# One of the two units of each expert matrix is fetched on ScalarE's queue, the other on SyncE's

## The reference

```python
hb = jax.nn.silu(xb @ w_gate[e]) * (xb @ w_up[e])
return (hb @ w_down[e]) * g[:, None].astype(x2.dtype)
```

## Time and profile before

| | us |
|---|---|
| median of 3 runs (1364.02 to 1364.54) | 1364.14 |
| the profiled execution's own time | 1364.34 |
| its span, first to last instruction | 1362.6 |
| PE busy | 1202.1 |
| ACT busy | 267.4 |

### The profile page before, as it was taken

One profiled execution on the slowest core, in us unless ns is written; L12 is line 12 of the kernel. 1 busy time (PEld: TensorE's weight loads), 2 busy tenths in 40 slices (PEclk: granted clock), 3 DMA queues, 4 the chain that ended last, 5 costly groups with the idle time before them and its releaser, 6 DMA issues.

```text
span 1362.6 us, 18400 instructions
## 1 busy us (share of the span) xinstructions
PE 1202.1 (88%) x7496; PEld 787.6 (58%) x7496; DVE 468.2 (34%) x1154; ACT 267.4 (20%) x687; POOL 323.7 (24%) x343
## 2 busy tenths in 40 slices
PE   7999999986856556676899999999999999999997
PEld 6865555452522121222286569999448666999843
DVE  3443434101011010101125646444573224444467
ACT  4313432010000000000224531111013222111100
POOL 5000100000000000000111348878001113987800
PEclk9999998988987787888999999999999999999999
DMA  9643345999999999999997135554343058644400
GB/s 349 196 176 124 124 183 210 425 428 423 429 427 426 430 428 428 430 425 424 407 314 258 39 106 187 173 186 155 128 151 123 0 167 266 207 149 172 155 0 31
DMA packets 101357, 335.82 MB, mean 246 GB/s; under 512 B 6728, under 2 KB 58240, under 8 KB 87069
## 3 DMA queue, kind: packets, MB, share of 16 engines
q1 hardware_dynamic: 98662, 326.33, 62.1%
q0 software_dynamic: 2416, 8.30, 1.7%
q10 hardware_dynamic: 199, 0.06, 0.0%
HBM read 333.59 MB, written 2.86 MB: 247 GB/s over the span
## 4 chain that ended last, share of the span: by engine, by line
PE 71%; DMA 18%; DVE 3%; POOL 3%; ACT 2%; issue 2%; SPq 1%; POOLq 0%; DVEq 0%; ACTq 0%
PE bank L1714 18%; PE bank L892 18%; DMA ring<-in_w_expert_up 11%; PE bank L1764 8%; PE bank L1248 5%; PE bank L1266 4%; DMA ring<-in_w_expert_down 2%; DMA ring<-in_w_expert_gate 2%; PE bank L1872 2%; DMA wide_rows<-in_w_expert_gate 2%; PE bank L1138 2%; PE bank L1685 2%; PE bank L1527 1%; PE bank L1500 1%; PE bank L1055 1%
## 5 line engine op out<-in xcount | busy, mean ns | idle before, releaser
L892 PE MATMUL bank<-wide_rows,ring 128*128 128x256 f32 (+3 forms) x592 | 129.9, 372 | 0.2 <-ACT ring L2014 0.2
L1714 PE MATMUL bank<-R,arena 128*128 128x128 f32 x1056 | 125.1, 275 | 0.0
L1248 PE MATMUL bank<-ring,arena 128*32 128x512 f32 x512 | 79.2, 711 | 49.8 <-DMA ring<-in_w_expert_up 38.5
L1714 PEld LDWEIGHTS bank<-R,arena 128*128 128x128 f32 x1056 | 121.5, 192 | 0.0
L892 PEld LDWEIGHTS bank<-wide_rows,ring 128*128 128x128 f32 (+1 forms) x592 | 107.5, 190 | 19.7 <-issue 3.9
L3189 POOL COPY arena<-w_router 128x256 f32<-128x256 f32 x1 | 0.4, 397 | 476.3 <-PE bank L1248 476.3
L2693 DVE TENSOR_TENSOR arena<-arena,bank 64x512 f32<-64x512 f32 x16 | 11.1, 691 | 294.9 <-ACT arena L2127 294.9
L1248 PE MATMUL bank<-wide_rows,arena 128*32 128x512 f32 x128 | 68.4, 686 | 47.4 <-DMA arena<-in_w_expert_up 35.6
L1714 PE MATMUL bank<-wide_rows,ring 128*128 128x128 f32 x704 | 91.3, 276 | 1.5 <-ACT wide_rows L2112 1.5
L1714 PEld LDWEIGHTS bank<-wide_rows,ring 128*128 128x128 f32 x704 | 84.7, 192 | 2.5 <-ACT wide_rows L2112 2.5
L1266 PE MATMUL bank<-ring,arena 128*32 128x512 f32 x504 | 72.5, 718 | 13.0 <-ACT arena L2130 10.1
(11 more groups left out here) (394 smaller groups left out, 1956.1 us busy)
## 6 DMA issues: line engine op xcount, KB each, us to landing
ring<-in_w_expert_down SPq DMA_DIRECT2D x29, 2048.0 KB, 16.1
ring<-in_ffn_w_in SPq DMA_DIRECT2D x44, 1024.0 KB, 7.8
ring<-in_w_expert_gate SPq DMA_DIRECT2D x16, 2048.0 KB, 25.0
ring<-in_w_expert_up SPq DMA_DIRECT2D x16, 2048.0 KB, 32.4
arena<-in_w_expert_up SPq DMA_DIRECT2D x14, 2048.0 KB, 32.6
ring<-in_ffn_w_out SPq DMA_DIRECT2D x10, 2048.0 KB, 7.8
ring<-in_w_in SPq DMA_DIRECT2D x7, 2048.0 KB, 15.8
arena<-in_w_expert_gate SPq DMA_DIRECT2D x7, 2048.0 KB, 26.5
```

What stands on the lines that cost most here:

```text
L892: last = pe.matmul(dst, lhsT, rhs, start=k == 0, stop=k == len(pairs) - 1)
L1248: last = pe.matmul(bank[e % 2][at:at + SLOTS, :], xg_tile(e % 2, k)[:, SLOTS * r:SLOTS * r + SLOTS], w[r][:, kk, :], start=k == 0, stop=k ...
L1714: last = pe.matmul(up_banks[layer][u % 4][i][:, at * P:(at + 1) * P], weights(k), columns(k), start=k == 0, stop=k == KT // 2 - 1)
```

## The change

From pair 3 on, SP issues only units 0, 2 and 4 of each pair (`of[::2]`, or `of[1::2]` where the list begins with an odd number), and ACT issues units 1, 3 and 5 in a new function `fetch`, each behind a wait with the same count as SP's had. ACT does so at four places of `moe_quad(i)`: behind the silu of pair 2i+1 (gate and up of pair 2i+3), behind the silu of pair 2i+2 (first down unit 5 of that same pair 2i+2, then gate and up of pair 2i+4), and behind the turned copy of pair 2i+2 (down unit 5 of pair 2i+3). In the last quad (i = 6) only down unit 5 of pair 14 is left. Pair 2, the halves of pair 15, unit 0 of pairs 3 to 6 and everything behind the experts stay on SP. Source, destination and semaphore of each transfer are the same.

```diff
--- before.py
+++ after.py
@@ -816,12 +816,12 @@
                 sp.dma_start(ring[:, base % RING, :] if in_ring else spare[0], expert(0, pair)).then_inc(place_of(0, pair % 2)[1], 16)
 
             def odd_pair(i, of=range(6)):
-                for u in of:
+                for u in of[::2] if of[0] % 2 == 0 else of[1::2]:
                     used_up(u, i * 2 + (0 if u < SPARES else 1))
                     next_unit(u, i * 2 + 1, u < SPARES)
 
             def even_pair(i, of=range(6)):
-                for u in of:
+                for u in of[::2] if of[0] % 2 == 0 else of[1::2]:
                     used_up(u, i * 2 + (1 if u < SPARES else 2))
                     next_unit(u, i * 2 + 2, False)
 
@@ -2158,16 +2158,38 @@
                     last = act.activation(late_memory[:, side], bank[2 + side][:, :].rearrange("p (b c) -> p b c", b=2), ACT.Copy)
                 last.then_inc(mem_staged, 1)
 
-            def moe_quad(i, first=False, memory=None):
+            base = first_unit["moe"]
+
+            def fetch(units_of, pairs, pair, spared):
+
+                for u in units_of:
+                    act.wait_ge(moe["down" if u >= 4 else "gate_up"], pairs * 2)
+                    src = {"gate": w_expert_gate, "up": w_expert_up, "down": w_expert_down}[DUO_UNITS[u]][0].rearrange("e (p k) n -> p e (k n)", p=P)
+                    if isinstance(pair, int):
+                        dst, src = (spare[u] if spared else ring[:, (base + u) % RING, :]), src[:, 2 * pair + 1, :]
+                    else:
+                        dst = (spare[u] if spared else ring[:, (base + u) % RING, :]).rearrange("p (e m) -> p e m", e=1)
+                        src = src[:, bass.ds(2 * pair + 1, 1), :]
+                    act.dma_start(dst, src).then_inc(spare_in[u] if spared else landed[(base + u) % RING], 16)
+
+            def moe_quad(i, first=False, memory=None, last=False):
                 if memory == 0:
                     mem_columns()
                 if memory is not None:
                     for side in range(2):
                         mem_out(2 * memory + side)
                 moe_silu(1, i, first)
+                if not last:
+                    fetch((1, 3), i * 2 + 2, i * 2 + 3, True)
                 moe_turned(1, i, first)
                 moe_silu(2, i)
+                if not first:
+                    fetch((5,), i * 2 + 2, i * 2 + 2, False)
+                if not last:
+                    fetch((1, 3), i * 2 + 3, i * 2 + 4, False)
                 moe_turned(2, i)
+                if not last:
+                    fetch((5,), i * 2 + 3, i * 2 + 3, False)
 
             moe_silu(0, 0, first=True)
             moe_turned(0, 0, first=True)
@@ -2187,7 +2209,7 @@
                             silu(r).then_inc(ov["silu"], 1)
                             act.wait_ge(ov["turned"], count)
                             turned(r).then_inc(ov["turned_copied"], 1)
-            moe_quad(LAST_QUAD)
+            moe_quad(LAST_QUAD, last=True)
             e = DUOS - 1
             moe_silu(e, 0)
             moe_turned(e, 0)
```

## The result

The changed kernel takes 1377.79 us (median of 4 runs, 1375.25 to 1380.25) against 1364.08 (4 runs, 1363.70 to 1364.54) of the kernel before on the same chip: ratio 1.0105 [1.0091, 1.0119], slower by 13.7 us. The forecast was 1368.2 us with a range of 1360.5 to 1375: the sign was right, the size was not. The profiled execution took 1378.93 us, its span is 1377.2, 14.6 us longer than before.

What follows compares the result with a forecast made beforehand. The prediction took transfer bytes over DMA rate to bound the expert stage. Its terms, 2.5 + 1.3 for the tail and 0.3 for the start, gave +4.1 us on 1364.14, so 1368.2 us, range 1360.5 to 1375.

Steps and rivals of the forecast that it cites:

- The bound: Expert stage, 265 to 671 us: time is bytes over rate, DMA engines busy without a gap at 426 GB/s.
- three ways: Kernel's end moves only by another rate, moments with all queues empty, or a longer tail from last need to landing.
- rival 2: Whole kernel: no change by rule, spreading issues saves only issue time, 1364.1 us; chance 0.25 together with hidden after all.
- Rival 3: Transfers of the expert stage: two queues fill small gaps, a higher rate gives 1359.4 us; chance 0.15.
- ACT's issues cost nothing: Even pairs, between silu and turned copy: three issues, 1.3 us, fit in ACT's 2.18 us of idleness, costed at 0.
- rival 4: ACT before the turned copy of even pairs 4 to 14: issues stall on a full queue, 1368 to 1390 us; chance 0.10.
- Rivals 1 and 2: Late unit hidden by the reserve (1365.8 us), or no change at all by rule (1364.1 us); chance together 0.25.
- A wait of 9.7 takes the place of one of about 9 us: Even pairs 4 to 12: PE's new wait for down replaces its gate and up wait, 0 us, ends 0 and +3.5.
- The tail, 2.5 + 1.3 = 3.8 us: Pair 14: down products 10.1 us late against 7.6 us of reserve, +2.5; slower products behind a longer wait, +1.3.
- The reserve: Pair 15's down halves: SP could issue them 7.6 us later before the engines ran empty.
- Half a rate for the late unit: Down unit 5 of even pairs: at equal shares with SP's full queue it lands 12.7 us after issue.
- The start, +0.3: Pairs 2 to 4: early requests delay pair 2's down units 10 to 17 us, mostly absorbed; +0.3 us, ends 0 and +6.5.

Runs made afterwards that it cites:

- e7: Changed kernel with all down units back on SP and ACT also fetching units 1 and 3 of pair 15 behind pair 13's silu: 1367.31 us.
- e11: Changed kernel, but ACT asks for its half at SP's old moments and in SP's old order, pair 15 too: 1373.65 us.
- e6: Changed kernel, but ACT also asks for the halves of units 1 and 3 of pair 15 behind pair 13's silu: 1377.59 us.
- e5: Changed kernel without the register loads and untaken branches to the overflow passes, on every engine: 1373.00 us.
- e15: Changed kernel with ACT fetching only from pair 7 on, pairs 3 to 6 by SP alone: 1377.94 us.
- e12: The kernel of e11 with ACT fetching only from pair 7 on, pairs 3 to 6 by SP alone: 1365.34 us.
- e9: Changed kernel with the edits of e1 and e6 together: 1377.63 us.
- e1: Changed kernel, but ACT asks for down unit 5 of even pairs ahead of the silu, behind the odd pair's turned copy: 1375.80 us.
- e4: Changed kernel, but down unit 5 of pair 14 alone is asked for ahead of its silu: 1376.89 us.

## Why the prediction was right in sign and wrong in size

- **The bound** held for the rate, but its list of three ways was too short. That "the order of data does not matter" (rival 2) was wrong: e7 loses 4.1 us with 0.6 us of holes. Rival 3 fell: from 405 to 600 us e11's two queues move 428 GB/s, as the kernel before does with one.
- **ACT's issues cost nothing** held: 0.34 to 0.38 us each in pair 8, turned copy after 2.13 us of idleness in place of 2.18. Three of the 36 took over 1 us (1.23 to 1.95), which was rival 4's sign, but behind that of pair 12 (1.43) the copy again starts after 2.18 us. Rival 4 fell. Rivals 1 and 2 fell as well, the loss being larger than forecast.
- **"A wait of 9.7 takes the place of one of about 9 us" at 0, at most +3.5: this is the step that failed.** The wait came as forecast (10.29 us, pair 8), and PE's later wait shrank. But the step's own condition, "the engines keep working", was taken as given. SP's next turn waits for the very products that are late, so its queue is dry for 12 us in pair 8 (478 to 490). Of the holes before 633, 5.2 us lie from 489 to 600 around such waits; "holes in the transfers in every even pair" had been my own sign of being wrong. The silu of pair 14 starts 6.7 us late, where the term was 0, at most 3.5. I had followed who waits for unit 5 on PE, and not who waits for PE on SP.
- **The last turn** was not in the sum: 7.1 us of hole at 633 to 642, because two of six units had gone out early and the last quad has no early request behind them. PE waits for no data from 613 to 648.7, so this hole is not in the 6.7 us, and e6, which fills it, wins nothing; the 5.2 us of the branch are, and I had not listed them as covered by a wait that the change removes. Without the branch (e5) that silu is 4.4 us late and the kernel 4.8 us faster.
- **The tail, 2.5 + 1.3 = 3.8 us**: from the silu of pair 14 to the end of its down products I had 18.4 us and 1.3 for the clock; it took 18.35 in all (648.73 to 667.08), 10.0 more than the 8.3 before. That part held, with 1.2 us for the clock (6.27 in place of 5.11). But behind it PE alone has 20.1 us of work to the end of pair 15's down products (667.1 to 687.2), where before 22.3 us passed (650.3 to 672.6) with a wait for data in them. The reserve was 22.3 - 20.1 = 2.2 us and not 7.6: I had computed it from the transfers and left PE's own road out. The term is 10.0 - 2.2 = 7.8 us, forecast as 3.8, and 6.7 + 7.8 = 14.5 us is the difference of the two spans (14.6). So the sum of 0 (steady part), 3.8 (tail) and 0.3 (start) stands against 6.7, 7.8 and nothing.
- **Half a rate for the late unit** gave 12.7 us where 12.67 and 11.94 were measured, by the wrong parts. In pair 14 q10 shows no packet before 652 us, 3.3 us after the request. Then, from 652 to 658 us:

```profile
q10 hardware_dynamic: 111, 1.82, 70.6%
q1 hardware_dynamic: 115, 0.82, 32.3%
```

  Equal numbers of packets, so two thirds of the engines for the 16 KB packets, 7.3 us for the unit: the rule of the Trainium skill (DMA: Bandwidth & Descriptors, section Queues, rings and completion order) that I had weighed and not followed. The sequence is 3.3 + 7.3 us and 1.4 us to landing; my fixed part of 2.9 us was too small by 1.8, and the two errors nearly cancelled. In pair 8 the parts differ again: both queues have 16 KB packets there and get 44 against 41 of them from 475 to 478, then SP's is empty; why that unit still takes 12.67 us isn't shown. The Trainium skill (same page, section Issuing engines are not separate DMA queues) says that a second issuing engine saves only issue time. The traces agree about the rate; on the order of the requests, which cost 1% here, that section says nothing.
- **The start, +0.3**: down of pair 2 ended 14.4 us late (10 to 17 forecast), and by pair 6 the silu is 1.1 us late; e15 shows no share of it in the end.

What stays open: the part of e12's 1.6 to 2.2 us that isn't the clock at pair 15, the 5 us in e6 beyond its holes, what else holds the end in e9, and why a queue with work waiting beside it shows its first packet only 3.3 us after the request.

## What to carry to other kernels

Before an issue is moved to another engine's queue, write down for each queue what wakes it and how many bytes it leaves behind at each wake; a request that comes later than before, or ahead of one that is needed sooner, is paid for even at a full rate. When a wait is moved, look for what lay under the old one (here a branch of 5 us), and at an end compute the reserve of every road, the engine's own work too: e1, e4, e6 and e9 each mended one or two roads and won 0 to 2 us.

## What was not expected of the hardware

Two hardware queues that both have work take turns by packets, not by bytes: 111 against 115 packets while the bytes stood 1.82 to 0.82 MB, and 70 against 78 packets (0.57 to 1.18 MB) in e7 from 624 to 628 us, there with the 8 KB packets on ScalarE's side. A new request beside a busy queue shows its first packet about 3.3 us after the issue (ScalarE's queue: none before 475.2 for the request at 472.02 in pair 8, none before 652.0 for that at 648.74 in pair 14). And leaving a loop past a register load and passes that are not run cost PE 5.2 us, with a fetch of instructions in them.
